# All 512-column matmuls of a weight piece ahead of its 256-column ones, in the stages with moving activations

## What is computed

```
h = rms_norm(x); x += silu(LN(dwconv31(glu(h @ w_in)))) @ w_out        # layer 0, mixer
h = rms_norm(x); x += diff_attention(h @ w_qkv) @ w_o                  # layer 1, mixer
h = rms_norm(x); x += (silu(dwconv3(h @ w_gate)) * (h @ w_up)) @ w_down  # after each mixer, F = 5504
return rms_norm(x)
```

## Time and profile before

| what | before |
|---|---|
| median of 3 runs | 2212.46 us (2209.05 to 2213.02) |
| the profiled execution's own time | 2210.5 us |
| its span, first to last instruction | 2208.7 us |
| TensorE matmul busy (PE) | 2164.4 us, 98% |
| TensorE weight load busy (PEld) | 1855.7 us, 84% |
| VectorE busy (DVE) | 1543.0 us, 70% |
| ScalarE busy (ACT) | 982.8 us, 44% |
| mean granted TensorE clock | 0.994 |

### The profile page before, as it was taken

The page is one execution under the profiler, slowest core; times in us unless marked ns, Lnnn a source line. Parts: engine busy times, 40 slices in busy tenths (PEclk is TensorE's granted clock), DMA queues, the critical chain, the costliest instruction groups (busy, mean ns, idle before and its releaser), DMA issues.

```text
span 2208.7 us, 32086 instructions
## 1 busy us (share of the span) xinstructions
PE 2164.4 (98%) x11198; PEld 1855.7 (84%) x11198; DVE 1543.0 (70%) x2521; ACT 982.8 (44%) x1408; POOL 31.9 (1%) x50
## 2 busy tenths in 40 slices
PE   8999799999999999999999999999999999999998
PEld 7888678888888888888888877788888888888886
DVE  5899976777777776454588866667777777764443
ACT  2111355444444444444444444455444444444443
POOL 5000000000000000000000000000000000000000
PEclk9999999999999999999999999999999999999999
DMA  7545355666666665555666554466666666656553
GB/s 224 152 135 150 115 167 177 190 190 189 188 186 188 185 189 197 194 187 186 186 174 187 171 172 153 153 191 177 187 189 189 190 190 189 189 192 206 201 188 109
DMA packets 561192, 395.86 MB, mean 179 GB/s; under 512 B 6343, under 2 KB 490705, under 8 KB 560849
## 3 DMA queue, kind: packets, MB, share of 16 engines
q1 hardware_dynamic: 560896, 395.01, 58.5%
q10 hardware_dynamic: 240, 0.08, 0.0%
HBM read 392.97 MB, written 2.10 MB: 179 GB/s over the span
## 4 chain that ended last, share of the span: by engine, by line
PE 86%; DVE 6%; issue 3%; SPq 2%; DVEq 1%; ACT 1%; DMA 0%; ACTq 0%
PE acc L1269 34%; PE acc L1274 17%; PE acc L1300 10%; PE acc L1302 10%; PE acc L1301 10%; DVE sb_part L822 4%; PE acc L1487 1%; PE acc L1489 1%; PE acc L1488 1%; SPq L313 1%; DVEq L90 1%; PE acc L1359 1%; PE aux L1316 0%; PE aux L1411 0%; DMA sb_stage<-in_conv_w_in 0%
## 5 line engine op out<-in xcount | busy, mean ns | idle before, releaser
L724 DVE TENSOR_TENSOR sb_w_lo<-sb_stage,sb_w_hi 128x1024 fp32r<-128x1024 f32 x680 | 827.1, 1217 | 462.0 <-ACT sb_w_hi L463 458.9
L1269 PE MATMUL acc<-sb_normed,sb_w_hi 128*128 128x512 f32 x3264 | 1027.4, 396 | 0.0
L463 ACT ACTIVATE sb_w_hi<-sb_stage 128x1024 fp32r<-128x1024 f32 x680 | 715.0, 1053 | 615.7 <-PE acc L1302 334.6
L1274 PEld LDWEIGHTS acc<-sb_normed,sb_w_lo 128*128 128x128 f32 x3264 | 613.1, 188 | 144.9
L1274 PE MATMUL acc<-sb_normed,sb_w_lo 128*128 128x256 f32 x3264 | 641.4, 278 | 0.0
L1269 PEld LDWEIGHTS acc<-sb_normed,sb_w_hi 128*128 128x128 f32 x3264 | 497.7, 189 | 0.6
L1300 PE MATMUL acc<-sb_w_hi,sb_hidden 128*128 128x512 f32 x688 | 267.9, 389 | 0.0
L1302 PE MATMUL acc<-sb_w_hi,sb_hidden 128*128 128x512 f32 x688 | 267.7, 389 | 0.0
L1301 PE MATMUL acc<-sb_w_lo,sb_hidden 128*128 128x512 f32 x688 | 267.7, 389 | 0.0
L1359 PE MATMUL acc<-sb_x_op,sb_stage 128*128 128x256 f32 x1024 | 225.6, 381 | 2.1 <-DMA sb_stage<-in_conv_w_in 2.1
L1359 PEld LDWEIGHTS acc<-sb_x_op,sb_stage 128*128 128x128 f32 x1024 | 195.5, 191 | 29.1 <-issue 1.6
(11 more groups left out here) (170 smaller groups left out, 1427.1 us busy)
## 6 DMA issues: line engine op xcount, KB each, us to landing
sb_stage<-in_ffn_w_gate SPq DMA_DIRECT2D x86, 1024.0 KB, 5.4
sb_stage<-in_ffn_w_up SPq DMA_DIRECT2D x86, 1024.0 KB, 5.4
sb_stage<-in_ffn_w_down SPq DMA_DIRECT2D x80, 1024.0 KB, 4.9
sb_stage<-in_attn_w_qkv SPq DMA_DIRECT2D x48, 1024.0 KB, 5.4
sb_stage<-in_conv_w_in SPq DMA_DIRECT2D x32, 1024.0 KB, 5.7
sb_stage<-in_conv_w_out SPq DMA_DIRECT2D x16, 1024.0 KB, 4.9
sb_stage<-in_attn_w_o SPq DMA_DIRECT2D x16, 1024.0 KB, 4.9
sb_stage<-in_ffn_w_down SPq DMA_DIRECT2D x8, 768.0 KB, 4.1
```

The source lines that it names most:

```text
L463: nc.scalar.activation(w_hi[:, (2 * first + h) % PIECES, 0:size], stage[:, first % STAGES, off:off + size], ACT.Copy).then_inc(hi_ready, 1)
L724: nc.vector.tensor_tensor(w_lo[:, slot, 0:size], stage[:, first % STAGES, off:off + size], w_hi[:, slot, 0:size].bitcast(F32), ALU.subtrac ...
L1269: nc.tensor.matmul(acc[:, bank, :], w_hi[:, slot, q * P:(q + 1) * P], operand[:, k, :], start=begin, stop=False, skip_group_check=True)
L1274: return nc.tensor.matmul(acc[:, bank, T:2 * T], w_lo[:, slot, q * P:(q + 1) * P], operand[:, k, 0:T], start=False, stop=end, skip_group_c ...
```

## The change

Within a piece the order of the sixteen matmuls is altered. Before, the piece went in groups of two tiles: two matmuls of 512 columns, then the two of 256 columns for the same tiles. Now all eight of 512 columns come first, and then all eight of 256. The waits, the count at the piece's last matmul, the buffers and the other engines are as they were. The diff in full:

```
                     slot = (2 * block_n + h) % PIECES
                     if h == 1 and halfway:
                         halfway()
-                    for q in range(0, KD // 2, 2):
-                        for p in (q, q + 1):
-                            for tile, count in arrivals:
-                                if tile == k + p:
-                                    pe.wait_ge(operand_ready, count)
-                            high_product(bank, slot, p, operand, k + p, k + p == 0)
-                        for p in (q, q + 1):
-                            ins = low_product(bank, slot, p, operand, k + p, k + p == KD - 1)
+                    for q in range(KD // 2):
+                        for tile, count in arrivals:
+                            if tile == k + q:
+                                pe.wait_ge(operand_ready, count)
+                        high_product(bank, slot, q, operand, k + q, k + q == 0)
+                    for q in range(KD // 2):
+                        ins = low_product(bank, slot, q, operand, k + q, k + q == KD - 1)
                     k += KD // 2
                     ins.then_inc(pieces_done, 1)
```

## The result

The changed kernel takes 2215.14 us (median of 19 runs, 2213.07 to 2217.06) against 2210.66 us (19 runs, 2208.87 to 2213.02), a ratio of 1.0017 with a 95% interval of 1.0011 to 1.0024. It is a little slower, by 3.8 us on the ratio (the interval is 2.4 to 5.3 us), where I forecast 8 us less. The time lies inside my range, but on the wrong side of no change. The three runs of before on which I had built have a median 1.8 us above that of all 19, so the forecast starts from too high a time; the change that it forecasts isn't touched by that.

A forecast was written before the change was run, and what follows sets the result against it. The prediction took TensorE's matmuls, busy 98% of the span, to bound the kernel. Its terms, -9.0 + 0 + 1.0 = -8.0 us, took 2212.46 to 2204.5 us, with a range of 2194 to 2218 us.

The forecast's parts named there:

- What bounds the kernel: TensorE, busy 98%; the ending chain runs over the 512- and 256-column matmuls, with 0.0 us of idle time before them.
- Term 1: 512-column matmuls in runs of eight: five at 232 ns, three at 227; 0.022 us less per piece, 9.0 us in all.
- Term 2: 256-column matmuls in runs of eight: 0.1155 us each as before, change 0; bounds 16 us more to 5 us less.
- rival 3: 256-column runs: overhead per instruction, 121 ns each, costs 16 us; sum +8 us, 2220.5 us; threshold about 118 ns; chance 0.18.
- Term 3: Second piece of the first block in up0, qk and up1: TensorE waits for tile 15, 1.0 us more in all.
- The sum: Whole kernel: -9.0 + 0 + 1.0 = -8.0 us, giving a median of 2204.5 us.
- Rivals 1 and 2: 1: 256-column runs also settle, 114 ns, 2199.5 us, chance 0.14; 2: order immaterial, only waits remain, 2213.5 us, chance 0.26.

The follow-up runs named there:

- One and one: Against the kernel before: one 512-column matmul, then one of 256, alternating, instead of groups of two; ten runs from 2207.45 to 2218.55 us, median 2216.39.
- Four and four: Against the kernel before: four matmuls of 512 columns, then four of 256, twice per piece, instead of groups of two; 2218.00 us, ratio 1.0036.

## Why the prediction was wrong

**What bounds the kernel** was right: the change in the stages went to the end, and no wait for weights appeared in steady blocks.

**Term 1**, the 512-column matmuls, was right in mechanism and in size: 1.84 us for eight, five of them unsettled and three at 227 ns, as read from the earlier trace rows. The gain was 24 ns per piece, 9.8 us, where I had 9.0.

**Term 2** is the step that failed, as a size: "eight take 8 x 0.1155 us as now, change 0". They take 0.953 us against 0.922 before, 0.031 us more per piece, 12.6 us over the 408 pieces. The price I gave for the overhead that belongs to the instruction, 121 ns, was nearly the right one (120); only the first matmul of a run, at 113, and the second, at 119, are cheaper. So the cost that rival 3 priced at 16 us was 12.6. The 0.115 us of the earlier trace rows isn't the price of a 256-column matmul but of one between changes of length, where start times shift between neighbours: a part of what the 256s cost shows up in the spacing of the 512s beside them. One and one shows it best: its spacings are 231, 112, 233 and 118 ns, none of them a settled one, and their sum is twice 226.7 + 120. I read start-to-start distances in a mixed stream as costs of single instructions. Only the sum over a cycle is a cost: 697 ns before, against 693.3 settled. With that sum my own count, 56 ns by the instruction against 57 found, spoke for rival 3, and I put it down at 0.18 and kept the middle.

That the overhead goes by the instruction was only one of two readings in the prediction, and is shown by the kernel with all matmuls of 256 columns, by the 120 ns of long runs and by the 173 ns at 384 columns.

**Term 3** was right in place and nearly in size: 0.87 us in the first blocks for 1.0 forecast. I had counted one stall, for tile 15; the load stalls for tile 14 also, and the two together cost 0.26 us in up0 where I had 0.3. Keeping the old order there gave the first blocks back.

**The sum** over steady pieces is thus -24 + 31 = +7 ns, some +2.7 us, and with the waits +3.6 us, about what the ratio shows (3.8). Seen from the settled prices: before, each four matmuls cost 3.3 ns over 693.3, or 13 ns a piece; in the new order one change to and fro costs 20 ns a piece over 2773. The longer runs did bring fewer changes, but each became dearer. Four and four pays 16.5 ns twice a piece, and one and one nothing in its short pattern but 53 ns a piece in its long one. So the price of a change depends on the whole pattern, and no rule found here gives it ahead of a run. That the measured time lies in my range says little for the forecast: the range was wide enough to take in a part of rival 3.

**The rivals.** Rival 3 is what happened in its mechanism, and its threshold of 118 ns was passed; it forecast +8 us, and since the first two 256s are cheaper and the 512s gained a little more, the time came out between that and no change. Rivals 1 and 2 fell: the 256s don't go at 114 ns, and the order does matter. The rule of the Trainium skill for an isolated gap (TensorE: Matmul & The Clock Gate, section Back-to-back issue gap), N / 2.4 + 2.5 ns, has the right slope for these fp32r matmuls, but the runs of one length show 13.3 ns in place of 2.5. For a real stream of loads and matmuls the same section of the Trainium skill gives 131 ns a matmul of 512 columns, which the prediction left out; the runs show 227, so this figure doesn't hold here either.

## What to carry to other kernels

In a mixed stream read the cost of a matmul from a whole cycle of the pattern, and the price of each kind from a long run of its own; a spacing between neighbours of different length isn't one. The most that regrouping could win here, if no cycle goes below the settled prices (none of these runs did), is 3.3 ns in 697, some 5 us in the whole kernel. So look first at how large that sum is. Where operands of a first block arrive late, the work that stands ahead of the wait is its cover: keep that block's order when you regroup the rest.

## What was not expected of the hardware

- At the full clock a settled fp32r matmul with its own weight load costs columns / 2.4 GHz + 13.3 ns: 120 ns for 256 columns and 227 for 512, both in streams of one length, and 173 for 384, seen only in the last two of runs of eight.
- A change of length unsettles the stream. Behind 256-column matmuls the 512s take 233, 236, 228, 232, 231 ns before they come to 227, and the first 256 behind settled 512s takes 113. What inside the engine does this is open; no run here looks into it.
- Alternating single matmuls of 512 and 256 columns have two stable patterns, 347 and 353 ns a tile. In the three profiles of one and one each stage of 86 blocks falls into one of them in its first two blocks and keeps it, and a stage is 8.9 us longer in the long one. The same program can thus differ by that much from one execution to the next.
